# Second block of a two-block model on one core: when the residual is scaled, where the step-size arithmetic stands, and which banks the gate tiles use

## The reference

```
h = rms_norm(x, norm_mix_g)
proj = h @ w_in     # z, xbc, dt_raw, q_a, kv_a, k_rope, gates
xbc = silu(causal_depthwise_conv(xbc, conv_w, conv_b))   # 4 taps
dt = softplus(dt_raw + dt_bias);  a = dt * -exp(a_log)
y = ssd_chunked_scan(xs*dt, a, B, C) + xs*d_skip   # chunks of 128
y = rms_norm(y * silu(z)) @ w_ssd_proj
x = x + (g_ssd*y + g_mla*mla(...)) @ w_o
x = x + ffn(rms_norm(x, norm_ffn_g))
```

## Time and profile before

| | us |
|---|---|
| median of three runs | 1690.99 |
| the profiled execution's own time | 1690.33 |
| its span in the profile | 1688.5 |
| TensorE busy | 1630.1 |
| VectorE busy | 1052.7 |
| ScalarE busy | 789.1 |
| GpSimd busy | 660.3 |

### The profile page before, as it was taken

One profiled execution on the slowest core, in us unless ns is written; L12 is line 12 of the kernel. 1 busy time (PEld: TensorE's weight loads), 2 busy tenths in 40 slices (PEclk: granted clock), 3 DMA queues, 4 the chain that ended last, 5 costly groups with the idle time before them and its releaser, 6 DMA issues.

```text
span 1688.5 us, 22330 instructions
## 1 busy us (share of the span) xinstructions
PE 1630.1 (97%) x7880; PEld 1286.9 (76%) x7899; DVE 1052.7 (62%) x1601; ACT 789.1 (47%) x1336; POOL 660.3 (39%) x307
## 2 busy tenths in 40 slices
PE   7999999999999799899999999999999999999999
PEld 6688777777887688676678876776778888888887
DVE  6599685777346676767778157777665676555200
ACT  5423465564253554566574246556543454444211
POOL 4244653233451344244353532222234344444442
PEclk9999999999998899999999999999999999999999
DMA  5233222123331333111113321111133232332331
GB/s 203 76 113 100 88 76 63 51 75 125 113 100 51 119 100 101 62 51 49 39 39 100 100 77 62 50 51 51 53 123 100 87 97 91 99 99 91 100 96 63
DMA packets 40119, 142.72 MB, mean 85 GB/s; under 512 B 4696, under 2 KB 5176, under 8 KB 39648
## 3 DMA queue, kind: packets, MB, share of 16 engines
q1 hardware_dynamic: 37600, 131.96, 24.7%
q10 hardware_dynamic: 2432, 9.59, 1.6%
HBM read 137.31 MB, written 4.21 MB: 84 GB/s over the span
## 4 chain that ended last, share of the span: by engine, by line
PE 79%; issue 9%; DVE 6%; ACT 4%; POOL 2%; ACTq 0%; POOLq 0%; DVEq 0%
PE bank L745 17%; PE bank L747 16%; PE bank L746 16%; PE bank L1348 4%; PE bank L1347 4%; PE bank L1349 4%; POOL w_lo L610 2%; PE bank L1236 2%; PE bank L797 1%; PE bank L798 1%; PE bank L796 1%; PE bank L1142 1%; PE bank L1257 1%; PE bank L1245 1%; PE bank L1204 1%
## 5 line engine op out<-in xcount | busy, mean ns | idle before, releaser
L610 POOL TENSOR_TENSOR w_lo<-w_raw,w_hi 128x1024 fp32r<-128x1024 f32 x243 | 594.9, 2451 | 988.0 <-ACT w_hi L1369 850.6
L745 PE MATMUL bank<-u_hi,w_hi 128*128 128x512 f32 x792 | 338.8, 428 | 21.3 <-DVE taps L2434 12.7
L747 PE MATMUL bank<-u_hi,w_lo 128*128 128x512 f32 x792 | 311.6, 393 | 0.0
L746 PE MATMUL bank<-u_lo,w_hi 128*128 128x512 f32 x792 | 311.3, 393 | 0.0
L1369 ACT ACTIVATE w_hi<-w_raw 128x1024 fp32r<-128x1024 f32 x199 | 209.3, 1055 | 211.0 <-PE bank L747 168.6
L745 PEld LDWEIGHTS bank<-u_hi,w_hi 128*128 128x128 f32 x792 | 150.2, 190 | 65.7 <-issue 13.9
L746 PEld LDWEIGHTS bank<-u_lo,w_hi 128*128 128x128 f32 x792 | 150.7, 190 | 33.5 <-issue 4.6
L747 PEld LDWEIGHTS bank<-u_hi,w_lo 128*128 128x128 f32 x792 | 150.0, 189 | 32.8
L1347 PE MATMUL bank<-u_hi,w_hi 128*128 128x512 f32 x288 | 112.0, 389 | 0.0
L1348 PE MATMUL bank<-u_lo,w_hi 128*128 128x512 f32 x288 | 112.0, 389 | 0.0
L1349 PE MATMUL bank<-u_hi,w_lo 128*128 128x512 f32 x288 | 112.0, 389 | 0.0
(11 more groups left out here) (472 smaller groups left out, 3469.6 us busy)
## 6 DMA issues: line engine op xcount, KB each, us to landing
w_raw<-weights SPq DMA_DIRECT2D x243, 512.0 KB, 3.5
xt<-x_t SPq DMA_DIRECT2D x8, 256.0 KB, 6.7
hank<-bias_dram ACTq DMA_DIRECT2D x8, 256.0 KB, 4.1
xt<-x_t ACTq DMA_DIRECT2D x1, 2048.0 KB, 8.7
h_dram<-h_res ACTq DMA_DIRECT2D x1, 2048.0 KB, 7.0
h_res<-h_dram ACTq DMA_DIRECT2D x1, 2048.0 KB, 8.0
out<-h_res SPq DMA_DIRECT2D x8, 256.0 KB
p_val<-p_t ACTq DMA_DIRECT2D x1, 512.0 KB, 10.8
```

The costliest lines, as they stand in the source:

```text
L610: pool.tensor_tensor(w_lo[:, j, :], w_raw[:, j, :], w_hi[:, j, :].bitcast(F32), ALU.subtract).then_inc(w_lo_ready, 1)
L745: pe.matmul(o, hi, xh, start=(i == 0), stop=False)
L746: pe.matmul(o, hi, xl, start=False, stop=False)
L747: mm = pe.matmul(o, lo, xh, start=False, stop=(i == n - 1))
```

## The change

Seven edits, all in the second block:

- VectorE no longer scales h_res before the convolution tiles. The unscaled h_res goes to DRAM, and with it the spread scale row, copied from bank 6 to `r_out`. ScalarE does the copy, both stores and the three loads of constants at i = 12 of its loop (`send_residual`). The row comes back as `r_back`, and in the loop over `mix_out` VectorE scales tile i of h_res just before it waits for the product that it adds.
- ScalarE's logarithms (`step_logs`) stand at i = 0 of its loop, after taps and weight parts of the first tile.
- VectorE's arithmetic is cut up and stands in its loop, after the product: step sizes at i = 0, two scans at 1, two scans and chunk ends at 2, the three parts of the stack at 6, 8 and 10.
- ScalarE's four exponentials and the chunk decay stand at i = 7.
- TensorE makes the product of the chunk ends after the third c tile, and the turned columns after the first x tile.
- At i = 20 ScalarE takes the sigmoid before the first group's copies and exponentials. The sigmoid stands behind the inserted steps of i = 0, 7, 10 and 12.
- z begins with bank 0 and then 1, and kva has bank 2.

```diff
-    plan.use_banks(1, 0)
-    for name, n, reader in (("z", 16, "D"), ("qa", 2, "A"), ("kva", 1, "A")):
+    plan.use_banks(0, 1)
+    for name, n, reader in (("z", 16, "D"), ("qa", 2, "A")):
         plan.columns(name, n, KD, reader)
+    plan.use_banks(2)
+    plan.columns("kva", 1, KD, "A")
...
                 column_tile(t, of_u2)
+                if t is st["ssd_c"][2]:
+                    pe.wait_ge(acum_ready, 1)
+                    pe.wait_ge(ends_ready, 1)
+                    pe.wait_ge(norm_std, 3)
+                    pe.matmul(bank[4][:, 0:2 * SSD_H], ones[0:SSD_H, 0:P], ends_diag[:, :], start=True,
+                              stop=True).then_inc(ends_spread, 1)
             pe.wait_ge(lo_ready, n_lo["u2"])
-
-            pe.wait_ge(acum_ready, 1)
+            column_tile(st["ssd_x"][0], of_u2)
+
             pe.wait_ge(dte_ready, NT)
...
-            for t in st["ssd_x"][:early]:
+            for t in st["ssd_x"][1:early]:
                 column_tile(t, of_u2)
 
             pe.wait_ge(consts2_in, 16 * 3)
             pe.wait_ge(cols_ready, 3)
+            pe.wait_ge(stack_a_ready, 1)
             spread_keys(0)
...
+            pe.wait_ge(e_ready, 16)
             column_tile(st["kva"][0], of_u2)
-            pe.wait_ge(e_ready, 16)
...
-            act.wait_ge(x2_ready, KD)
-            act.dma_start(h_dram, h_res[:, :, :].rearrange("p a b -> p (a b)")).then_inc(h_spilled, 16)
...
+            def send_residual():
+
+                act.wait_ge(norm_spread, 3)
+                act.copy(r_out[:, :], bank[6][:, :]).then_inc(r_copied, 1)
+                act.wait_ge(r_copied, 1)
+                act.dma_start(r_dram, r_out[:, :]).then_inc(h_spilled, 16)
+                act.dma_start(h_dram, h_res[:, :, :].rearrange("p a b -> p (a b)")).then_inc(h_spilled, 16)
+                for dst, name in ((one_hot, "one_hot"), (trig, "trig"), (tri_b, "tri_b")):
+                    act.dma_start(dst[:, :], a[name]).then_inc(consts2_in, 16)
...
-                if i == 2:
+                if i == 0:
+                    step_logs()
+                if i == 7:
 
                     act.wait_ge(acum_ready, 1)
                     for c in range(NT):
                         act.activation(r_dte[:, c * P:(c + 1) * P], r_ac[:, c * P:(c + 1) * P], ACT.Exp, scale=-1.0,
                                        bias=r_ac[:, (c + 1) * P - 1:(c + 1) * P]).then_inc(dte_ready, 1)
+                    act.wait_ge(ends_spread, 1)
+                    act.activation(chunk_decay[:, :], bank[4][:, 0:2 * SSD_H], ACT.Exp).then_inc(cols_ready, 1)
...
+                if i == 12:
+                    send_residual()
+                if i:
+                    act.wait_ge(dve_freed, conv_tiles[i - 1][0]["freed"][1])
+                    act.activation(taps_sg[:, (i - 1) % 2, :], taps[:, (i - 1) % 2, :], ACT.Sigmoid).then_inc(conv_sg, 1)
                 if i == len(conv_tiles) - 4:
 
-                    act.wait_ge(stack_a_ready, 2)
+                    act.wait_ge(stack_a_ready, 1)
                     act.wait_ge(cols_ready, 3)
                     group_out(0)
                     key_decays(0)
-                if i:
-                    act.wait_ge(dve_freed, conv_tiles[i - 1][0]["freed"][1])
-                    act.activation(taps_sg[:, (i - 1) % 2, :], taps[:, (i - 1) % 2, :], ACT.Sigmoid).then_inc(conv_sg, 1)
...
+            act.dma_start(r_back[:, :], r_dram).then_inc(h_back, 16)
...
-            dve.wait_ge(norm_spread, 3)
-            for i in range(KD):
-                dve.scalar_tensor_tensor(h_res[:, i, :], h_res[:, i, :], vec("norm_final", i), bank[6][:, :], ALU.mult,
-                                         ALU.mult).then_inc(x2_ready, 1)
-            dve.wait_ge(x2_ready, KD)
...
+                if i == 0:
+                    steps_and_rates()
+                elif i == 1:
+                    running_sums(0, 2)
+                elif i == 2:
+                    running_sums(2, 4)
+                    chunk_ends()
+                elif i == 6:
+                    first_part()
+                elif i == 8:
+                    second_part()
+                elif i == 10:
+                    third_part()
...
+                dve.scalar_tensor_tensor(h_res[:, i, :], h_res[:, i, :], vec("norm_final", i), r_back[:, :], ALU.mult,
+                                         ALU.mult).then_inc(x2_ready, 1)
+                dve.wait_ge(x2_ready, i + 1)
                 dve.wait_ge(dense_done, t["full"])
                 free(dve.tensor_tensor(h_res[:, i, :], h_res[:, i, :], bank[t["bank"]][:, :], ALU.add))
```

More of the change, by code:

```diff
@@ L474, in build @@
         h_dram = nc.dram_tensor("h_dram", (P, KD * S), F32).ap()
+        r_out = at("r_out", 136, [P, S])
+        r_dram = nc.dram_tensor("r_dram", (P, S), F32).ap()
+        r_back = at("r_back", 198, [P, S])
         o_hi = [at(f"o_hi{i}", kb, [P, S], F32R) for i, kb in enumerate((166, 168, 202, 204, 186, 188, 190, 192))]
@@ L523, in build @@
         stack_a_ready = sem("stack_a_ready")
+        ends_ready = sem("ends_ready")
         dte_ready = sem("dte_ready")
@@ L572, in build @@
         act_sg = sem("act_sg")
+        r_copied = sem("r_copied")
         hg_hi_ready = sem("hg_hi_ready")
@@ L1025, in _ @@
             mm.then_inc(cols_turned, 1)
[L1027 to L1030, removed]
             def spread_keys(p):
@@ L1698, in _ @@
             high_parts(lambda i: u2_hi[:, i, :], lambda i: val_f[:, i % 2, :], KD)
-            act.wait_ge(x2_ready, KD)
-            act.dma_start(h_dram, h_res[:, :, :].rearrange("p a b -> p (a b)")).then_inc(h_spilled, 16)
-            for dst, name in ((one_hot, "one_hot"), (trig, "trig"), (tri_b, "tri_b")):
-                act.dma_start(dst[:, :], a[name]).then_inc(consts2_in, 16)
             t = st["small2"][0]
@@ L1708, in _, with step_logs @@
             after(t)
[L1710 to L1714, removed]
+            def step_logs():
+                act.wait_ge(act_freed, st["small2"][0]["freed"][1])
+                link(act.activation(r_t2[:, :], small2[0:SSD_H, :], ACT.Abs))
+                link(act.activation(r_t2[:, :], r_t2[:, :], ACT.Exp, scale=-1.0))
+                act.activation(rate[:, :], vecs[0:SSD_H, VEC["a_log"][0]:VEC["a_log"][0] + 1],
+                               ACT.Exp).then_inc(rate_ready, 1)
+                act.activation(r_t2[:, :], r_t2[:, :], ACT.Ln, bias=1.0).then_inc(dt_log, 1)
+            def send_residual():
[6 more added lines that the diff above has]
+                    act.dma_start(dst[:, :], a[name]).then_inc(consts2_in, 16)
             def key_decays(p):
@@ L1761, in _ @@
                              ).then_inc(cols_ready, 1)
-                    act.wait_ge(cols_ready, 1)
+                    act.wait_ge(cols_ready, 2)
                     for c in range(NT):
@@ L2442, in spread_col @@
                 return cols[:, i, h0:h0 + n].unsqueeze(2).broadcast_to([P, n, SSD_P])
[L2445 to L2466, removed]
+            def steps_and_rates():
+                dve.wait_ge(dt_log, 1)
+                dve.wait_ge(rate_ready, 1)
+                link(dve.scalar_tensor_tensor(r_dt[:, :], small2[0:SSD_H, :], 0.0, r_t2[:, :], ALU.max, ALU.add))
+                link(dve.tensor_scalar(r_t2[:, :], r_dt[:, :], rate[:, :], -1.0, ALU.mult, ALU.mult))
@@ new lines, in running_sums, with chunk_ends @@
+            def running_sums(first, end):
+                for c in range(first, end):
+                    ins = dve.tensor_tensor_scan(r_ac[:, c * P:(c + 1) * P], ones[0:SSD_H, 0:P],
+                                                 r_t2[:, c * P:(c + 1) * P], 0.0, ALU.mult, ALU.add)
+                    link(ins)
+            def chunk_ends():
+                dve.sem_inc(acum_ready, 1)
+                for c in (1, 2):
+                    ins = dve.tensor_scalar(ends_diag[:, (c - 1) * SSD_H:c * SSD_H], ident[0:SSD_H, 0:SSD_H],
+                                            r_ac[:, (c + 1) * P - 1:(c + 1) * P], None, ALU.mult)
+                ins.then_inc(ends_ready, 1)
@@ new lines, in first_part, with second_part, third_part @@
+            def first_part():
+                link(dve.tensor_copy(stack_a[0:32, :], r_ac[:, :]))
+                link(dve.tensor_tensor(r_n2[:, :], r_ac[:, :], stack_a[0:32, :], ALU.subtract))
+            def second_part():
+                link(dve.tensor_copy(r_p2[:, 0, :], r_n2[:, :]))
+                link(dve.tensor_copy(stack_a[32:64, :], r_p2[:, 0, :]))
+            def third_part():
+                link(dve.tensor_tensor(r_n2[:, :], r_n2[:, :], r_p2[:, 0, :], ALU.subtract))
+                dve.tensor_copy(stack_a[64:96, :], r_n2[:, :]).then_inc(stack_a_ready, 1)
@@ L2635, in gate_used @@
                                          ALU.mult).then_inc(gates_used, 1)
-            dve.wait_ge(h_spilled, 16)
+            dve.wait_ge(h_spilled, 32)
             b0 = VEC["gate_b"][0]
@@ L2712, in _ @@
```

(2 more changed lines are left out.)

2 lines of the change are left out of this document (removed).

## The result

The changed kernel takes 1673.43 us (median of 4 runs, 1672.62 to 1675.27), the kernel before 1690.95 (4 runs, 1690.77 to 1695.9): ratio 0.9893, 95% interval 0.9878 to 0.9908. The profiled run took 1674.19 (span 1672.4); before 1690.33 (1688.5). So 16.1 us of span are to be explained (17.5 by the medians); 18.8 were forecast.

A forecast was written before the change was run, and what follows sets the result against it. TensorE, busy 97% of the span, was the bound, so only its stalls and low clock could yield time. 13.6 + 5.2 = 18.8 off 1690.33 gave 1671.5, plus 0.66 beside the median 1672.2 us; range 1670 to 1674, wider 1669.0 to 1677.5.

The forecast's parts named there:

- Parts 1 to 3: Convolution tiles up to the first x tile: stalls and low clock gone, 13.3 us, cross-check 13.8, taken as 13.6.
- Part 1: Residual stored unscaled: small2 starts 543.0, not 552.5; the 1.89 us wait before tile number 3 and low clock go, 3.6 us.
- part 2: VectorE's step-size and decay arithmetic among the tiles: the 8.21 us wait before tile number 4 and low clock go, 9.7 us.
- Part 3: Tile number 7: exponentials ready 4.35 us after it ends, transposes come 5.45 us after; slack 1.1 us.
- rival B: After the first x tile, transposes wait for ScalarE: 1 to 2 us plus about 1.6 of low clock; chance 0.07.
- Part 4: Last tiles, new order: z0 starts 17.3 us after tile number 20 ends; gain 5.2 us, between 3 and 6.1.
- Part 5: Last-product stage: eight scalings of 0.74 us fit VectorE's idle time before each add; cost 0.
- Part 6: Banks of qa and kva, and the wait for e moved before kva: nothing waits there, 0.
- D: From b0 to z1: unbroken matmuls lower the clock without idling, slower than before, 1691 to 1701 us; chance 0.02.

The follow-up runs named there:

- scaling early: Changed kernel with the eight residual scalings back on VectorE ahead of the tiles, ScalarE not waiting for them: 1674.43 us, ratio 0.99.
- the two loads: Changed kernel with two more table switches (an Exp and a Sigmoid) on ScalarE ahead of the four exponentials at i = 7: 1679.18 us, ratio 0.9925.
- the inverse was moved: Changed kernel with the first half of VectorE's reciprocal moved from ahead of the last pair's weights to ahead of the group's third gate product: 1668.54 us, ratio 0.9861.
- issues early: Changed kernel with the unscaled residual's spill and two of three constants issued ahead of small2, without waiting for a scaling: 1675.18 us, ratio 0.9905.
- old banks: Changed kernel with only the banks of the gate tiles and kva, and kva's place before the last wait, as before: ratio 0.9908.
- block with early exponentials: Changed kernel with logarithm and VectorE's step-size chain in one block ahead of the tiles, the four exponentials at i = 1 instead of 7: ratio 0.9913.
- head wait with early exponentials: Changed kernel with scaling ahead of the tiles, ScalarE's wait and issues ahead of small2, and the four exponentials at i = 4 instead of 7: ratio 0.9918.
- the block's kernel: Changed kernel with the logarithm and VectorE's whole step-size chain in one block ahead of the tiles: 1680.31 us, ratio 0.9931.
- both old parts: Changed kernel with both the order at the last tiles and the banks as before, only the head changed: ratio 0.9935.

## Why the prediction was right

Point by point, with the predicted figure first.

- *Parts 1 to 3:* 13.6 against 13.06. The waits and the low clock at b3 and c0 are gone, nothing took their place. 0.3 of the difference stand there before the edited stretch: b1 starts at 543.96, and before the change at 543.70.
- *Part 1's small2 at 543.0, logarithm to 550.9, b0's taps at 545.4:* 543.13, 551.0 and 545.47, by ScalarE's and VectorE's timelines of the changed kernel:

```profile
543.13 0.69 ACT L1712 ACTIVATE small<-bank,vecs 128x512 f32<-128x512 f32 x1 [4.41 <-PE bank L778]
...
550.38 0.63 ACT L1722 ACTIVATE r_t<-r_t 32x512 f32<-32x512 f32 x1
```
```profile
545.47 2.32 DVE L2453 SCALAR_TENSOR_TENSOR taps<-bank,vecs,taps 128x511 f32<-128x511 f32 x3 [5.96 <-ACT taps L1768]
...
555.58 0.85 DVE L2474 TENSOR_TENSOR_SCAN r_ac<-ones,r_t 32x128 f32<-32x128 f32 x2
...
678.62 0.69 DVE L2537 TENSOR_TENSOR xdt<-bank,cols 128x512 f32<-128x512 f32 x1
...
1278.95 0.74 DVE L2770 SCALAR_TENSOR_TENSOR h_res<-h_res,vecs,r_back 128x512 f32<-128x512 f32 x1
```

- *3.6 for part 1 and 9.7 for part 2:* right as prices of two stalls in the kernel before, wrong if read as what each half is worth. Alone, each half delayed the tiles by a wait of 2 us only, and the place of the exponentials, safe with both halves done, turned it into 7 to 8. The ring takes up a delay of several microseconds once; of two in a row the second is paid.
- *Part 1's cause:* I named the scaling, the wait and the issues. The scaling early is free, and so are the issues while ScalarE waits for the pair. What costs is the chain of them, ScalarE waiting for the scaling and issuing behind it; how much is the wait's and how much the issues' no run separates, and by the estimate above it took both.
- *Part 3, slack 1.1:* 1.0 by the two loads. That is little: rival B did not fire in the changed kernel, but it did in both kernels whose tiles started late and whose exponentials stood at number 7, and in the one with two more loads.
- *Part 4:* 5.2 against 18.23 minus 13.06, 5.17. z0 started 17.2 after x12's end (17.3 forecast), the waits for the scaled values came to one of 0.20 us where I had feared 0.9; VectorE's first of them at 678.62 was in time for the slots between the matmuls of z1, and z0 and z1 ran on at clock 1.00.
- *Part 5:* the scaling is one operation of 0.74 in idle time, and TensorE has no wait in that stage. 0, as said. *Part 6:* 0; nothing in the list of waits belongs to it.
- *The sum:* 18.8 against 16.1 (own time 1671.5 against 1674.19). The edited stretch gave 18.2. What I put at nothing without a reason is a change in the price of stalls that stay: 1.4 us at 857 and about 0.6 in attention, by the clock. Two of the four runs are at 1672.6 and may have been spared one of them; they have no profile. The forecast of 1672.2 lies within the runs, but that it is only 1.2 under the median is partly luck: run again, the changed kernel gained 14.9 us and not 17.5, under the 17.0 to 21.0 that the narrower range of 1670 to 1674 means, though within the wider one up to 1677.5.
- *Rivals:* none of the four occurred in the changed kernel. D's claim that the clock may fall without idle time is not borne out: 68.1 us at 1.00.

What stays open: why the same stall of some 2 us is followed by the lower clock in one program and not in the next, and what ScalarE's wait for the scaling costs without the issues behind it. No run here was made for either.

## What to carry to other kernels

Where a ring of buffers couples two engines, look first at what stands ahead of the first tile on each in-order queue, and above all at waits for work that a later stage needs, and at what is issued behind such a wait; arithmetic and DMA issues in a slot where the engine waits anyway are free. A stall has no price of its own: two delays that the ring would nearly absorb singly can cost more than their sum, or less, so undo parts both alone and together before giving each a figure. And when a change has emptied one region, read the list of waits again: the next 4 us here were one instruction moved past a wait.

## What the runs showed of the hardware

- *Two-input work of VectorE beside GpSimd.* Four scans took 6.03 us in one block beside two GpSimd subtractions of 2.4 us, and 0.85 per pair among the tiles. The Trainium skill's page SBUF — State Buffer (section SBUF: two separate sides) calls the shared ports an exclusive lock, held for the whole instruction; the trace agrees in the product of a tile, 1.71 beside GpSimd's subtraction and 0.69 alone. GpSimd is started by ScalarE's high part, so in a late kernel the product meets it at every tile, and the loop stays at 4.85 us.
- *The clock after a short stall.* After 1.91 us at b3 the granted clock was 0.66 over 5 us in one kernel and 1.00 in another with the same text up to there and the same wait; after 1.95 us for weight_b it was 1.00 before the change and 0.79 to 0.87 after. That wait, 1.94 to 1.96 us long, is in 13 of the 14 profiles (not where the inverse was moved). Over the 5 us behind it the clock was 0.66 to 0.69 in six of them (the changed kernel, its repetition, scaling early, issues early, old banks, block with early exponentials) and 1.00 in the other seven. Two of the 13 have it 0.07 us apart: first the block with early exponentials (wait to 856.82), then the head wait with early exponentials (to 856.75), columns as in the earlier trace rows:

```profile
856.80:861.80 5.00, 4.68 (x24) 4.04 (x25) 4.75 (x5) 0.00 (x1) 2.37 (x2) 0.69 0.01 3
```
```profile
856.80:861.80 5.00, 4.70 (x31) 3.95 (x32) 4.90 (x6) 0.00 (x0) 2.29 (x2) 1.00 0.01 3
```

So neither the length of the stall nor its time decides it. Where the clock falls it costs 1.4 to 1.7 us behind most stalls, nearly as much as one of 2 us; behind 3.4 us in the block's kernel it was 2.7, and behind 4.51 us it was 1.6 before the change and 3.0 with both old parts. Figures from one profile below some 2 us carry this uncertainty.
